# Value products of two pairs of attention units issued together in every second step, with eight buffers for the transposed probabilities

## What is computed

```python
def memory_attention(mq, mem_n, w_kv, mq_g, mk_g):   # 4 heads x 64, 256 memory tokens
    ...
    p = jax.nn.softmax(logits, axis=-1).astype(mv.dtype)
    out = jnp.einsum('bhsm,bmhd->bshd', p, mv)
```

## Time and profile before

| | |
|---|---|
| median of 3 runs | 1865.03 us (1864.84 to 1866.87) |
| profiled execution | 1864.26 us, span 1862.3 us |
| mean granted clock | 0.998 of full speed |
| PE busy / PEld / DVE / ACT / POOL | 99% / 87% / 64% / 53% / 36% of the span |
| chain that ended last, largest entry | PE bank L685, 15% |
| DMA | 277.21 MB, mean 149 GB/s |

### The profile page before, as it was taken

How to read it: one execution, slowest core, us unless ns; L and a number is a source line. 1 busy time by engine, 2 the same in 40 slices (tenths; PEclk the granted TensorE clock), 3 DMA queues, 4 the chain that set the end, 5 groups by cost and what they waited for, 6 DMA issues and landing times. The chain is left out here.

```text
span 1862.3 us, 33686 instructions
## 1 busy us (share of the span) xinstructions
PE 1849.0 (99%) x11709; PEld 1629.4 (87%) x11709; DVE 1183.3 (64%) x1925; ACT 994.1 (53%) x1610; POOL 671.1 (36%) x530
## 2 busy tenths in 40 slices
PE   9999999999999999999999999999999999999999
PEld 7999988887778899998889999888877788999887
DVE  6999821368753999951088998114787459899311
ACT  6444554565666544454474445546657564444642
POOL 2366611112511166631115666111226012666210
PEclk9999999999999999999999999999999999999999
DMA  8433398878337633378874334988781485333885
GB/s 229 122 106 98 115 216 192 187 186 193 78 92 179 149 113 97 106 184 200 187 175 111 95 111 129 209 193 198 179 211 33 100 205 130 105 99 112 203 187 141
DMA packets 78085, 277.21 MB, mean 149 GB/s; under 512 B 8624, under 2 KB 10928, under 8 KB 77744
## 3 DMA queue, kind: packets, MB, share of 16 engines
q1 hardware_dynamic: 48960, 175.67, 30.0%
q0 software_dynamic: 28464, 98.05, 29.6%
q10 hardware_dynamic: 576, 2.36, 0.4%
HBM read 175.91 MB, written 2.10 MB: 96 GB/s over the span
## 5 line engine op out<-in xcount | busy, mean ns | idle before, releaser
L557 POOL DMA_DIRECT2D w_lo<-raw x179 | 153.9, 870 | 774.4 <-ACT w_lo L1257 735.3
L629 POOL TENSOR_TENSOR w_lo<-s_sum,w_hi 128x512 fp32r<-128x512 f32 x200 | 321.9, 1623 | 239.7 <-ACT w_hi L1305 239.7
L1256 ACT ACTIVATE w_hi<-raw 128x1024 fp32r<-128x1024 f32 x155 | 164.0, 1058 | 337.4 <-PE bank L685 321.8
L685 PE MATMUL bank<-t_hi,w_hi 128*128 128x256 f32 x1152 | 326.3, 283 | 3.6 <-DVE zf L1785 3.6
L685 PE MATMUL bank<-t_lo,w_hi 128*128 128x256 f32 x1152 | 326.0, 283 | 0.0
L685 PE MATMUL bank<-t_hi,w_lo 128*128 128x256 f32 x1152 | 326.0, 283 | 0.0
L685 PE MATMUL bank<-a_hi,w_hi 128*128 (+1 forms) x832 | 324.6, 390 | 0.0
L685 PE MATMUL bank<-a_lo,w_hi 128*128 (+1 forms) x832 | 323.8, 389 | 0.0
L1305 ACT ACTIVATE w_hi<-s_sum 128x512 fp32r<-128x512 f32 x216 | 127.7, 621 | 274.5 <-DVE s_sum L1767 268.5
L685 PE MATMUL bank<-a_lo,w_lo 128*128 (+1 forms) x704 | 273.9, 389 | 0.0
L1697 DVE TENSOR_TENSOR a_hi<-zf,a_lo (+1 forms) x88 | 63.5, 726 | 322.2 <-ACT a_lo L1365 322.2
(11 more groups left out here) (212 smaller groups left out, 3886.5 us busy)
## 6 DMA issues: line engine op xcount, KB each, us to landing
raw<-weights SPq DMA_DIRECT2D x326, 512.0 KB, 4.2
w_lo<-raw POOLq DMA_DIRECT2D x179, 512.0 KB, 6.2
x<-x_t SPq DMA_DIRECT2D x4, 512.0 KB, 7.1
t_lo<-t_sum POOLq DMA_DIRECT2D x4, 512.0 KB, 5.9
b_lo<-hn POOLq DMA_DIRECT2D x4, 512.0 KB, 7.3
mem<-mem_t ACTq DMA_DIRECT2D x2, 1024.0 KB, 8.1
out_t<-x SPq DMA_DIRECT2D x8, 256.0 KB, 2.1
const<-consts SPq DMA_DIRECT2D x1, 481.5 KB, 9.2
```

The lines of the kernel that those rows point to most:

```text
L557: G.dma_start(w_lo[:, s], raw[:, s], accum_op=ALU.add).then_inc(w_ready[pos], 16)
L629: G.tensor_tensor(out=fast_weight(l, e, product, 0, True), in0=s_sum[i - 1][:, :], in1=fast_weight(l, e, product, 0, False).bitcast(f32), ...
L685: return nc.tensor.matmul(out_, lhsT, rhs, start=start, stop=stop, skip_group_check=True)
L1256: nc.scalar.activation(w_hi[:, s], raw[:, s], ACT.Copy).then_inc(w_hi_done, 1)
```

## The change

The value products are issued only in steps n that are divisible by 4, from step 8 on, for two pairs of units at once: V(n - 8), then V(n - 6). In the steps between (6, 10, 14, ...) there is none. Eight tiles `pt` take the place of four, the new ones in tiles 8 to 11 (the first half of `h_lo`), and a copy of unit n waits for the V of unit n - 8.

```diff
+PT = 8
...
-    pt = [place(f"pt{i}", T, h_at + i * tile_b) for i in range(4)]
+    pt = [place(f"pt{i}", T, h_at + (i % 4 + 2 * (i - i % 4)) * tile_b) for i in range(PT)]
...
-        if n >= 4:
-            eng.wait_ge(pv_done[n % 2], l * (UNITS // 2) + (n // 2 - 1))
-        copy(pt[n % 4][:, 0:blocks * P], bank[2 + n % 2][:, 0:blocks * P])\
+        if n >= PT:
+            eng.wait_ge(pv_done[n % 2], l * (UNITS // 2) + ((n - PT) // 2 + 1))
+        copy(pt[n % PT][:, 0:blocks * P], bank[2 + n % 2][:, 0:blocks * P])\
...
-                                      pt[(n + half) % 4][:, b * P:(b + 1) * P], b == 0, b == blocks - 1)
+                                      pt[(n + half) % PT][:, b * P:(b + 1) * P], b == 0, b == blocks - 1)
...
-                    if 0 <= n - LAG - 2 < UNITS:
+                    if n % 4 == 0 and n >= LAG + 4:
+                        times_v(n - LAG - 4)
                         times_v(n - LAG - 2)
```

## The result

The change makes the kernel slower by about 3 us. Twenty runs of each: 1867.82 us median (1866.26 to 1870.72) against 1865.11 (1863.33 to 1867.13); ratio 1.0017, 95% interval 1.0011 to 1.0023. A second set of runs gave 1.0024 (1.0015 to 1.0033).

A forecast was written before the change was run, and what follows sets the result against it. PE, busy 99% of the span, was taken as the bound. Added holds of 5.7 us less 1.3 saved gave 4.4 us (2.2 a layer), so 1865.0 + 4.4 = 1869.4 us, range 1865.4 to 1871.6.

The forecast's parts named there:

- rival (b): Holds in steps 8 and 20 don't come, the five old ones cost V's pairs: about 1.3 us a layer, 1867.6; chance 0.20.
- A lone V: V alone after T, in steps 6, 18, 30, 42: joining another V saves 0.16 us each, 0.6 a layer.
- Step 32: Attention step where a pool_map of 1 us covers; V(24) saves 0.16, bringing the delay to 0.95 us.
- d: The delay of PE against the kernel before, carried to the end of each attention step; forecast 2.2 us a layer.
- Step 8: L(8) waits for unit 6's mask, T(5) for unit 3's copy, with two V's behind: delay 0.4 us.
- Step 20: L(20) waits for unit 18's mask, T(17) for unit 15's copy: a new hold, delay from 0.3 to 0.8 us.
- Steps 36, 40, 44: T already held by DVE, moved V's behind it cost their pairs in full: 0.44, 0.44, 0.22; step 36 also loses step 32's saving.
- Step 16: T(13) already held by a chain; V(8) behind it adds 0.44, the chain ends 0.1 earlier: delay 0.3 us.
- The waits: PE's waits for the DVE copy were to grow from four to ten or more, from 1.6 us to several.
- Rival (a): Not slower: PE's shape changes decide, DVE and ACT keep up, lone V's save 0.16 each: 1863.8; chance 0.14.
- rival (c): More holds: V's moved in steps 12 and 24 are held too, 1.5 us a layer more, 1872.4; chance 0.06.
- steps 12 and 24: V joins another V, 0.87 us either way in step 12; the copy is early, so the delay stays unchanged.

The follow-up runs named there:

- e5_first_ahead: The changed kernel with V(n - 8) issued ahead of T and V(n - 6) behind it; attention stage 57.53 / 59.01 us in layers 1 / 2.
- l_change: The changed kernel with DVE's split_y put one step later; attention stage 56.58 / 56.56 us, ratio to the kernel before 0.9999.
- l_before: The kernel before with DVE's split_y put one step later; attention stage 55.19 / 55.20 us, median 1863.02 us, ratio 0.9987.
- n_joined: Kernel before, V moved only from the eight steps with an S before it, POOL's pooling sums and scaling left out; attention stage 57.37 / 57.33 us.
- e2_lone: Kernel before with only the lone V's of steps 6, 18, 30 and 42 moved; attention stage 59.08 / 58.81 us, ratio 1.0030.
- n_lone: Kernel before, V moved only from steps 6, 18, 30 and 42, POOL's pooling sums and scaling left out; attention stage 57.45 / 57.41 us.
- e1_buffers: Kernel before with the eight buffers alone, V's issued in the old order; attention stage 56.61 / 56.41 us against 56.45 / 56.42.
- n_before: The kernel before with POOL's windowed pooling sums and their scaling left out; attention stage 56.30 / 56.27 us.
- e3_joined: Kernel before with V moved only from the eight steps where it stood behind an S; attention stage 58.20 / 58.00 us, ratio 1.0013.

## Why the prediction was right

The forecast was slower by 4.4 us, the range 1865.4 to 1871.6; measured 1867.82, with 2.7 us between the medians and 3.2 by the ratio, 2.1 to 4.3. The direction and the mechanism held; the size by the stages is 4.2. The total alone would not show that: 1867.82 lies just under the likeliest case (1868.0 to 1871.0) and almost on rival (b)'s 1867.6, and only the stages and the rows tell the two apart. By the prediction's own bound of 0.2% the measured 0.17% counts as "within", to which it gave 0.45, and the interval reaches over the bound.

- *A lone V costs 1.03 us, a joined one 0.87; only four a layer are lone.* Right: 1.89 for two V's of 8 pairs, 0.2 from T or S to L. Step 32, the one lone V without a hold, took d from 0.89 to 0.73.
- *Step 8, 0.4.* Measured 0.40 in both layers, and in every kernel that moves V(0) behind the T of step 8.
- *Step 20, a new hold, 0.5.* Measured 0.49.
- *Steps 36, 40, 44: V's pairs in full.* 0.59, 0.44 and 0.21 against 0.6, 0.44 and 0.22. That this is cover is shown for step 40 by e5_first_ahead (0.00) and by l_change, which takes the chain away (0.00 against l_before), and for step 44 by e5_first_ahead (0.03). In step 36 e5_first_ahead still loses 0.34, and l_change 0.44 against l_before, as its hold stays.
- *Step 16, "the chain ends 0.1 earlier than before".* This is the term that was mis-sized: d fell by 0.27 where I had 0.1. The split itself began 0.12 earlier, as worked out, but took 0.69 us in place of 0.88, since it began 0.1 before the end of POOL's operation (508.05) instead of 0.3 before it. I had taken 0.88 for its length, and had not looked at POOL's rows. This 0.17 to 0.2 is the whole difference from there to the end. The rows of the changed kernel:

```profile
507.02 1.03 POOL L573 TENSOR_TENSOR wb<-wa 128x510 f32<-128x510 f32 x1
```

```profile
507.92 0.69 DVE L2130 TENSOR_TENSOR a_lo<-yt,a_hi 128x512 fp32r<-128x512 f32 x1
```

- *The waits* for a copy grew from 4 to 8, not to the ten or more that were forecast; 4 for masks came beside them, so that 12 waits make 5.0 us in all. Some holds stand inside a row and are not listed as waits: the six T's of step 16 span 1.21 us, against 0.88 without a hold.
- Rival (a), shapes alone, is out by the new waits, and by n_joined, which saves no change of shape and has no lengthened split, and yet costs 1.07 us. (Its sum, 1865.0 - 1.3, is 1863.7 and not 1863.8.) Rival (b), no hold at steps 8 and 20, is out by their rows. For rival (c), steps 12 and 24 show d unchanged, so no.

Not tried: another way for the two engines to share the copies, which would change the load of ACT.

## What to carry to other kernels

Before moving work off its place on the bound engine, look at what it stands in front of: if the next instruction is held by a chain of other engines, the moved work was free there and is not free behind it. A saving per change of shape counts only where the shape really goes away; here that was four of twelve places. And where such holds exist, shorten the chain first: one operation put behind the copy that PE waits for gained 2.5 us by the stages (2.0 by the medians), where regrouping PE's own list lost 4.2.

## What the runs showed of the hardware

- A DVE tensor_tensor with both inputs in SBUF that starts during a POOL tensor_tensor ends 0.3 us (256 columns) or 0.55 us (512) after it: up to 1.54 us in place of 0.69. Where it falls is set by offsets of a few tenths between engines, so that a small edit elsewhere can cost 1 us: e2_lone against n_lone is 1.6 us in one stage. The other way round, a POOL tensor_tensor that started 0.07 us after such a split took 1.51 us in place of 1.03. A POOL tensor_scalar did not hold the split up (0.43 us inside one of 1.52).
- PE's clock fell to its lower level for about 3.4 us, at 391 us in the profiled executions of both kernels, and at 1317 us in that of the changed one, where it cost 1.5 us. It stands at 1316 us in e1_buffers and n_before too, and at neither place in e3_joined, so it does not belong to the change. PE was busy for all of the stretch at 1317 us (3.50 of 3.50 us, granted clock 0.52). What makes it fall is not shown.
